# A decoder step with gathered experts: the first tile routed in four parts, the last part gathered as pairs of rows

## What is computed

```
h  = x + W_out( sigmoid(g_A) * SWA(n) + sigmoid(g_B) * GLA(n) ),   n = RMSNorm(x)
x' = h + PEER(n2),   n2 = RMSNorm(h);   then the final RMSNorm

PEER, for each token t, 8 heads:
  q      = n2 @ Wq                                  (16 sub-queries of 128)
  s      = q . sub-keys                             (16 score rows of 128)
  val,idx= top 16 of each score row
  sv     = top 16 of the pairwise sums of the two halves of a head  -> expert numbers
  g      = softmax(sv)
  out    = sum over 8 x 16 experts of  g * gelu(u[e] . n2) * v[e]
```

## Time and profile before

| | |
|---|---|
| median of 3 runs | 3785.92 us (3781.08 to 3799.24) |
| profiled execution | 3796.31 us |
| its span, first to last instruction | 3794.4 us |
| mean granted TensorE clock | 0.863 |
| busy share: TensorE matmul, VectorE, GpSimd, ScalarE | 76%, 74%, 64%, 19% |
| moved by DMA | 1298.82 MB, mean 342 GB/s |

### The profile page before, as it was taken

One profiled execution on the slowest core, in us unless ns is written; L12 is line 12 of the kernel. 1 busy time (PEld: TensorE's weight loads), 2 busy tenths in 40 slices (PEclk: granted clock), 3 DMA queues, 4 the chain that ended last, 5 costly groups with the idle time before them and its releaser, 6 DMA issues.

```text
span 3794.4 us, 33054 instructions
## 1 busy us (share of the span) xinstructions
PE 2893.8 (76%) x10012; PEld 1804.1 (48%) x10012; DVE 2803.8 (74%) x5629; ACT 726.4 (19%) x1673; POOL 2434.8 (64%) x2076
## 2 busy tenths in 40 slices
PE   8888589788787998888997768888777555555555
PEld 6777566456553665544663445455654211111111
DVE  0641788887788767877879897887889766766665
ACT  1321113322111133222121112322111110001001
POOL 0000176887667747766766777787667777777776
PEclk9899899899899997998999889988989767766668
DMA  4124399999999998999999999999999999999999
GB/s 150 45 90 171 126 403 402 349 355 405 420 401 350 412 345 313 335 348 383 387 409 349 362 344 413 394 337 378 421 406 355 351 351 362 413 385 366 373 368 364
DMA packets 342240, 1298.82 MB, mean 342 GB/s; under 512 B 39480, under 2 KB 48720, under 8 KB 321936
## 3 DMA queue, kind: packets, MB, share of 16 engines
q0 software_dynamic: 297216, 1082.26, 74.5%
q1 hardware_dynamic: 44848, 214.44, 14.6%
HBM read 1278.87 MB, written 19.76 MB: 342 GB/s over the span
## 4 chain that ended last, share of the span: by engine, by line
POOL 35%; PE 23%; DVE 15%; issue 12%; DMA 12%; DVEq 2%; ACT 1%; PEld 0%; ACTq 0%; SPq 0%; PEldq 0%; POOLq 0%
POOL ringb L600 35%; PE bank L867 9%; DMA ringb<-in_v,eidx 8%; PE vsum L777 5%; DVE ringb L1366 4%; PE bank L1064 3%; DVE acc L1408 2%; PE bank L907 2%; DVE scT L1779 1%; PE bank L923 1%; DMA wring<-in_w 1%; DMA ringb<-in_u,eidx 1%; PE bank L948 1%; DVE idx L1577 1%; DVE idx L1569 1%
## 5 line engine op out<-in xcount | busy, mean ns | idle before, releaser
L600 POOL DMA_INDIRECT ringb<-in_u,eidx x1024 | 1220.8, 1192 | 937.8 <-DVE eidx L1474 457.9
L777 PE MATMUL vsum<-ringb,diag 128*128 128x512 f32 x2164 | 1284.3, 737 | 615.2 <-DMA ringb<-in_v,eidx 567.4
L600 POOL DMA_INDIRECT ringb<-in_v,eidx x1024 | 1190.8, 1163 | 399.9 <-issue 300.0
L1366 DVE CUSTOM_DVE_ANT_0 ringb<-ringb,n2t 128x1024 f32<-128x1024 f32 x1032 | 1234.7, 1224 | 156.6 <-DMA ringb<-in_u,eidx 91.7
L777 PEld LDWEIGHTS vsum<-ringb,diag 128*128 128x128 f32 x2164 | 463.0, 229 | 1317.2 <-issue 1154.4
L1408 DVE SCALAR_TENSOR_TENSOR acc<-ringb,wgt,acc 128x1024 f32<-128x1024 f32 x483 | 620.7, 1285 | 326.6 <-DMA ringb<-in_v,eidx 315.9
L867 PE MATMUL bank<-wring,nTb 128*128 128x256 f32 x3024 | 681.4, 386 | 31.6 <-DMA wring<-in_w 28.0
L867 PEld LDWEIGHTS bank<-wring,nTb 128*128 128x128 f32 x3024 | 544.7, 182 | 171.2 <-DMA wring<-in_w 33.1
L1102 ACT ACTIVATE diag<-cst,wgt 128x128 f32<-128x128 f32 x541 | 207.6, 397 | 809.7 <-PE vsum L777 670.0
L907 PE MATMUL bank<-nTb,wring 128*128 128x256 f32 (+1 forms) x1152 | 263.0, 387 | 6.0 <-DMA wring<-in_w 3.2
L907 PEld LDWEIGHTS bank<-nTb,wring 128*128 128x128 f32 x1152 | 223.3, 194 | 59.9 <-issue 20.8
(11 more groups left out here) (254 smaller groups left out, 2276.1 us busy)
## 6 DMA issues: line engine op xcount, KB each, us to landing
wring<-in_w SPq DMA_DIRECT2D x152, 1024.0 KB, 7.8
ringb<-in_u,eidx POOLq DMA_INDIRECT x1024, 6.5
ringb<-in_v,eidx POOLq DMA_INDIRECT x1024, 6.5
n2t<-scratch_n SPq DMA_DIRECT2D x16, 512.0 KB, 7.5
oab<-in_xp SPq DMA_DIRECT2D x4, 1024.0 KB, 6.9
bTb<-in_keysT SPq DMA_DIRECT2D x4, 1024.0 KB, 11.3
vgb<-in_xp SPq DMA_DIRECT2D x4, 1024.0 KB, 8.9
scratch_h<-vgb SPq DMA_DIRECT2D x4, 1024.0 KB
```

What stands on the lines that cost most here:

```text
L600: pool.indirect_dma_start(out=ring[r], out_offset=None, in_=a["u"] if kind == "u" else a["v"], in_offset=bass.IndirectOffsetOnAxis(ap=at, ...
L777: last = mm(out[:, g * 512:(g + 1) * 512], lhs, ring[r][:, g * 512:(g + 1) * 512], start=(x == first), stop=(x == end))
L1366: v.tensor_tensor_reduce(out=ring[r], in0=ring[r], in1=n2t[:, n % 2, :], scale=1.0, scalar=0.0, op0=ALU.mult, op1=ALU.add, accum_out=dg[:, ...
```

## The change

- **Four parts.** The first tile is routed in four parts of two heads. After every fourth sub-query of block 0, VectorE runs `route_tile` and `gates` for two heads, and GpSimd may gather their experts. 20 quads (`EARLY`) run beside the rest of block 0. Block 1 then takes quads 20 to 120.
- **The late tile of block 0.** Its scores are no longer searched beside the matmuls: ScalarE copies them to `late_s`, and VectorE runs the 16 `best` of that tile at the start of block 1, beside `fm`.
- **Pieces.** The experts of tiles 6 and 7 are gathered from a new table `uv` in HBM whose rows hold `u` and `v` of one expert (8 KB). One gather brings 1 MB. There are 12 pieces: six in buffers that block 3 no longer needs (`wring` twice, `nTb`, `arena`, `qkb`, `n2t`), six in the ring. In this part the sums follow the dot products two steps behind (`SHORT`), and gelu is applied every 2 slots. Before it, six steps (`DRAIN`) carry the last 24 `v` rows of the old kind and no `u` rows.
- **h and n2 of block 3** stay in SBUF (`vog`, `oa`); their two stores and the loads `n2t` and `acc` of tiles 6 and 7 go. The sums of these tiles are made in place of `h`.
- Marks: block 3 now takes steps 248 to 386. The last step with work is 523 of a new count.

```diff
+SHORT = 2
+PIECES = 12
...
+HP = 2
+PARTS = PH // HP
+EARLY = 20
...
+WHOLE = SEG_OF[FIRST[NCH - 1]]
+QW = SEG_QUAD[WHOLE]
+XW = 2 * QW
+
+
+DRAIN = LAG // 2
+STEPS = QU + DRAIN + SHORT
+QUADS = STEPS + TAIL
+DOT_STEP = [a if a < QW else a + DRAIN for a in range(QU)]
+SUM_STEP = [a + DRAIN + SHORT if a >= QW else a + LAG if a + LAG < QW else QW + (a + LAG - QW) // 2 for a in range(QU)]
...
+SEG_GSIZE = [2 if i >= WHOLE else GROUP for i in range(len(SEGS))]
...
+    if c == 0:
+        for q in range(HC + 1):
+            out += [(("q", q), 4)] + ([(("rp", q // 4 - 1, i), 4) for i in range(3)] if q and q % 4 == 0 else [])
+        return out
...
-        return {k: 0 for k, _ in stages(c)}
-    lo = 0 if c == 1 else SEG_QUAD[SEG_OF[FIRST[c - 1]]] - MARGIN
-    hi = SEG_QUAD[SEG_OF[FIRST[c]]] - MARGIN
+        late = [k for k, _ in stages(c)]
+        late = late[late.index(("rp", 0, 2)) + 1:]
+        return {k: 1 + (EARLY - 1) * late.index(k) // len(late) if k in late else 0 for k, _ in stages(c)}
+    lo = EARLY if c == 1 else SEG_STEP[SEG_OF[FIRST[c - 1]]] - MARGIN
+    hi = SEG_STEP[SEG_OF[FIRST[c]]] - MARGIN
     total, done, out = sum(w for _, w in stages(c)), 0, {}
...
-    for c in range(1, NCH):
+    for c in range(NCH):
         last = None
         for (key, _) in stages(c):
             if last:
                 for q in range(MARKS[c][last], MARKS[c][key]):
-                    rate[q] = BY_PE[last[0]]
+                    rate[q] = BY_PE[last[0]] if c else 2.0
...
+        late_s = arena[:, 2304:2304 + HC * NK].rearrange("p (q n) -> p q n", q=HC)
+        late_tmp = bTb[:, 1920:2048].rearrange("p (t n) -> p t n", t=1)
...
+        flat = wring[:, :, :, :].rearrange("p w k c -> p (w k c)")
+        piece = [flat[:, 0:2 * D], flat[:, 2 * D:4 * D], nTb[:, 0:2 * D], arena[:, 0:2 * D], qkb[:, 0:2 * D],
+                 n2t[:, :, :].rearrange("p i d -> p (i d)")] + [ringb[:, r * D:(r + 2) * D] for r in FREED]
+        assert len(piece) == PIECES
...
-        STORES = [1 + (c == SC) for c in CC]
+        STORES = [(1 + (c == SC)) * (c < NCH - 1) for c in CC]
...
+        def sums_of(i):
+
+            R = NS if SEGS[i] == "S" else P
+            return vog[:, tile_at(SEGS[i])[1], :] if i >= WHOLE else acc[0:R, i % 2, :]
...
+            whole = q in DOTS and DOTS[q] >= QW
+            rows = [("u", 2 * DOTS[q] + j) for j in range(2)] if q in DOTS else []
+            rows += [("v", 2 * at + j) for at in SUMS[q] if at < QW for j in range(2)]
             for kind, x in rows:
                 i, k = ITEMS[x]
-                r, n = PLACE[(kind, x)]
-                if kind == "u" and k == 0:
+                if kind == "u" and i == 0 and k % (HP * TOPK) == 0:
+                    pool.wait_ge(picked.sem, picked.at((0, 0, k // (HP * TOPK))))
...
+                if whole:
+                    s, n = (x - XW) % PIECES, (x - XW) // PIECES
+                    if n:
+                        pool.wait_ge(piece_used[s], 2 * n)
+                    elif s == PIECES - RING // 2 - 1:
+                        row_used(pool, ("u", XW - 1))
+                    elif s >= PIECES - RING // 2:
+                        for r in range(2):
+                            r += FREED[s - (PIECES - RING // 2)]
+                            pool.wait_ge(slot_used[r], OLD_USES[r])
+                    pool.indirect_dma_start(out=piece[s], out_offset=None, in_=a["uv"], in_offset=place).then_inc(piece_here[s], 16)
+                    continue
...
+                        if c == 0:
+                            quads(1)
+                quads(MARKS[c][("rt", 0)] if c else EARLY)
...
+                            mm(room(pe, ("s1", c, m))[:, 0:P], qh[:, m % 2, P:2 * P], keysT[:, m, :], start=True, stop=True)\
+                                .then_inc(full.sem, full.did(("s1", c, m)))
...
+                    if c == 0 and q:
+                        copy(late_s[:, q - 1, :], ("s1", c, q - 1), filled(act, ("s1", c, q - 1))[:, 0:P])
+                        if q % 4 == 0:
+                            beside("rp", q // 4 - 1, 2)
+                            route_exp(c, 0, P, q // 4 - 1)
...
+                if i >= WHOLE:
+                    n2 = oa[:, tile_at(SEGS[i])[1], :]
...
+                    if c == 1:
+                        dve.wait_ge(late_ready, 1)
+                        for q in range(HC):
+                            best(dve, late_s[:, q, :], 1, P, 1, q, None, late_tmp)
+                            if q % 2:
+                                gap()
...
+                    best(dve, filled(dve, key), CH[c] if c else 1, P, 0, q, key, tmp)
+                    if c == 0 and q % 4 == 3:
+                        part, steps = q // 4, [0]
+                        if part == 0:
+                            dve.wait_ge(d_hs, stored(0))
+
+                        def gap_part():
+                            if steps[0] in (0, 3, 5):
+                                beside("rp", part, min(2, steps[0] // 2))
+                            steps[0] += 1
+
+                        route_tile(dve, 0, 0, P, gap_part, part)
+                        gates(dve, 0, 0, P, part)
+                if c == 0:
+                    continue
...
+                if c < NCH - 1:
+                    dve.wait_ge(d_hs, stored(c))
...
+        "uv": f(np.concatenate([x["peer_u"][0], x["peer_v"][0]], axis=1)),
```

More of the change, by code:

```diff
@@ L420, in build @@
         nT = nTb[:, :].rearrange("p (k t) -> p k t", k=KC)
+        qbT, kbT = (qkb[:, i * HB * CM:(i + 1) * HB * CM].rearrange("p (h t) -> p h t", h=HB) for i in range(2))
         vaS, kSn = vkS[:, 0, :], vkS[:, 1, :]
@@ L489, in build @@
         both = [(c, t) for c in CC for t, _ in tiles_of(c)]
+        routes = [(0, 0, part) for part in range(PARTS)] + both[1:]
         d_cst, d_par = sem("d_cst"), sem("d_par")
@@ L544, in build @@
         slot_used = [sem(f"slot_used{r}") for r in range(RING)]
+        piece_here = [sem(f"piece_here{r}") for r in range(PIECES)]
+        piece_used = [sem(f"piece_used{r}") for r in range(PIECES)]
         d_n2 = [sem(f"d_n2{i}") for i in range(2)]
@@ L614, in pool_program @@
             pool.sem_inc(init, 1)
-            for q in range(QU + LAG):
+            for q in range(STEPS):
                 pool_quad(pool, q)
@@ L754, in pe_quad @@
         def pe_quad(pe, q):
-            if not 0 <= q - LAG < QU:
-                return
             mm = nc.tensor.matmul
-            for j in range(2):
-                x = 2 * (q - LAG) + j
+            for x in [2 * at + j for at in SUMS[q] for j in range(2)]:
                 i, k = ITEMS[x]
@@ L774, in pe_quad @@
                     lhs, out = diag[:, diag_number[x] % DIAGS, :], vsum[:, :]
-                r = row_here(pe, ("v", x))
+                row = row_here(pe, ("v", x))
                 for g in range(2):
-                    last = mm(out[:, g * 512:(g + 1) * 512], lhs, ring[r][:, g * 512:(g + 1) * 512], start=(x == first), stop=(x == end))
-                last.then_inc(slot_used[r], 1)
+                    last = mm(out[:, g * 512:(g + 1) * 512], lhs, row[:, g * 512:(g + 1) * 512], start=(x == first), stop=(x == end))
+                last.then_inc(used(("v", x))[0], 1)
                 if x == end:
@@ L888, in beside @@
                 def beside(*point):
-                    if c:
-                        quads(MARKS[c][point])
+                    quads(MARKS[c][point])
                 beside("norm", 0)
@@ L1078, in pe_program @@
                         last.then_inc(full.sem, full.did(("sR", g)))
-                for i in range(12):
+                for i in range(12 if c else 0):
                     beside("rt", i)
@@ L1403, in dve_quad @@
                     dve.wait_ge(d_h[i % 2], 16 * (i // 2 + 1))
[L1404 to L1405 removed]
                 dve.wait_ge(wgt_ready, m + 1)
[L1407 to L1411 removed]
+                row, y = row_here(dve, ("v", x)), sums_of(i)
@@ L1413, in route_tile @@
+                STT(y, row, wgt[:, m % 2, at:at + 1], y, ALU.mult, ALU.add).then_inc(used(("v", x))[0], 1)
+        def route_tile(dve, c, t, R, gap, part=None):
             v = nc.vector
             TT = v.tensor_tensor
[L1415 to L1418 removed]
@@ new lines, in route_tile @@
+            scratch = small if part is None else small0
+            cut = lambda lo, n: scratch[0:R, lo * n_p:(lo + n) * n_p]
+            some = lambda lo, n: cut(lo, n).rearrange("p (a h k) -> p a h k", a=n, h=n_h)
+            xf = cut(0, 2).rearrange("p (q k) -> p q k", q=2 * n_h)
+            piu, pif, pij, e01 = some(2, 4).bitcast(u32), some(6, 4), some(10, 2), some(12, 2)
+            posu = cut(14, 1).bitcast(u32).rearrange("p (h k) -> p h k", h=n_h)
+            vv = val[0:R, t, 2 * h0:2 * (h0 + n_h), :].rearrange("p (h c) k -> p h c k", c=2)
@@ L1440, in route_tile @@
             gap()
-            for h in range(PH):
+            for h in range(n_h):
                 v.max(sv[:, h, 8:16], cd2[:, h, :])
```

245 lines of the change are left out of this document (136 added, 109 removed).

## The result

The changed kernel takes 3743.93 us in the median of four runs (3736.41 to 3753.17). The kernel before, run beside it, takes 3792.58 us (3781.08 to 3815.6). The ratio is 0.987 (0.982 to 0.991): 1.3% faster, where 3741 us and 1.2% were forecast. The total is right. It is right because two of its terms were wrong in opposite directions: the early start (A) gave nothing that can be measured, and the pieces (B) gave more than forecast, nearly twice as much in the profiled execution.

A forecast was written before the change was run, and what follows sets the result against it. The DMA engines, hardly idle once gathers start, were taken to bound the kernel, VectorE block 1. Profiled 3796.3 - 7 - 38 = 3751 us, or 3741 us against the 3785.9 median; 8 in 10 range 3690 to 3798 us.

The forecast's parts named there:

- A: Early start in block 0: gathers start 68 us earlier, most of it paid back by block 1's end; gain 7 us.
- B: Last part: 11 us from removed stores and loads, 33 from 8 KB rows, less 6 at the end; gain 38 us.
- Start of the gathers: Block 0: first gather at about 392 us, 68 us earlier; routing one part takes 9.3 us.
- End of block 0: Block 0 ends at 504 us, 44 us later than before, with 20 quads done.
- Block 1: VectorE sets it: 600 us busy plus 75 idle, taken as 680; ends at 1184 us instead of 1191.
- rival 3: Block 1 keeps 731 us, set by its engine chains; A gives -44 us, total 3792; 10%, 6% with Rival 1 too.
- A piece: Last part: each gather of 8 KB rows takes 2.66 us, 256 take 681 us for 714; gain 33 us.
- the forecast's own sign of being wrong: The forecast is wrong if block 1 takes 640 or 720 us, or a piece 2.5 or 2.8 us.
- rival 2: Last part: deep queues absorb the disturbance; a piece costs 2.47 us, B gives 87, total 3692 us; 12%.
- Rival 1: Last part: bytes bind, not packets; a piece costs 2.79 us, B gives 5, total 3774 us; 20%.
- changeover: Six DRAIN steps, and six more steps beside block 3: the DMA is full either way, so no cost.
- The end: After the last landing: 6 us longer (2 to 12), about 16 us to the end.

The follow-up runs named there:

- the half rows: Changed kernel with two gathers per piece from the joined table, each bringing only 2 KB after a buffer's first use: 1.021 of the kernel before, 3888.18 us.
- the new dot product in the last part: Changed kernel with two 4 KB gathers per piece from u and v, and scalar-tensor-tensor dot products in the last part: 0.990 of the kernel before, 3765.68 us.

## Why the forecast came true, and where it didn't

**Start of the gathers: right.** First gather at 394.6 us (392), a part's route 9.9 us (9.3). That is 66 us earlier than before.

**End of block 0: 7 us late.** The norm of block 1 starts at 512 us (504 to 505 forecast). The four routes were costed well; GpSimd and VectorE waited more for each other in between.

**Block 1: the step of A that failed.** Forecast were 600 us of VectorE's work plus 75 of its other waits, taken as 680 in all. Measured are 586.55 busy and 104.5 idle in 691 us: 85% and not over 86%. The work was put 13 us too high, and the idle time too low by 30. The waits for rows, which the sum took as gone, fell from 44.7 to 14.9 us:

```profile
DVE acc L1509 <- DMA ringb<-in_v,eidx: 12.2, 7, 3.2
DVE ringb L1464 <- DMA ringb<-in_u,eidx: 2.7, 3, 1.3
```

But the other idle time, which I had kept at 75, became 90. I had treated it as a constant of the mixer, and it isn't one: on the first chip it is 80 us for the pieces alone and 90 to 93 in the three kernels with the early start; on the third chip it is 98 without and 94 with it. That fewer quads beside the mixer leave more of VectorE's waits for TensorE and ScalarE unfilled would fit the first pair and not the second; it is not shown, and the cause stays open. The outcome lies between the forecast and rival 3, which named the mechanism (the mixer keeps part of its pace) with a block 1 of 731 us. A gave -10 us in the profiled execution, where +7 was forecast, and -5 (not distinguishable from 0) in the runs beside the pieces alone; by the traces of that pair block 1 ends 4 us later with it, on the third chip 3 us. So of 66 us of earlier start nothing measurable reached the end.

**A piece: the step of B that failed.** Forecast 2.66 us, measured 2.48 to 2.50, 426 GB/s in 560 us on end; 2.5 was the forecast's own sign of being wrong. By the forecast's own sum, 256 x (2.79 - 2.48) = 79 us in place of 33. The number is that of rival 2 (2.47), the reason is not. Rival 2 let deep queues absorb slow transfers; no slow transfers were there to absorb. I had the chain reversed: not "slow transfers hold GpSimd up while it writes descriptors", but VectorE's operations hold GpSimd, and the queues get less than they could move. A piece halves the gathers, GpSimd has 2.48 us for 1.71 of work, and with that all of the disturbance goes from 3150 us on, and not a third of it. Rival 1 (bytes bind at 2.79) fell with the half rows. The clue was in the rows: GpSimd followed itself at 0.30 us in the last part, also where the rate was low. An engine that never waits is the pace, whatever the DMA share says. (Of the four windows that the forecast put at 419 to 427 GB/s three are so, in rows 4; the one of rows 3 is 414.)

**What the sum of B missed besides.** 79 + 11 - 6 would be 84 us; about 70 came. The changeover costs about what is missing:

```profile
3066.00:3150.00 84.00, 48.44 (x79) 13.71 (x80) 55.45 (x92) 14.48 (x36) 49.44 (x32) 0.76 0.89 362
3080.00:3090.00 10.00, 7.91 (x19) 1.53 (x17) 2.01 (x2) 0.00 (x0) 3.18 (x3) 1.00 1.01 427
3100.00:3110.00 10.00, 6.12 (x10) 2.20 (x11) 9.93 (x16) 1.48 (x6) 7.95 (x2) 0.83 0.65 243
3110.00:3120.00 10.00, 3.21 (x7) 0.87 (x5) 4.55 (x9) 0.49 (x2) 8.78 (x5) 0.99 0.40 142
...
3078.39 0.94 POOL L676 DMA_INDIRECT ringb<-in_uv,eidx  x1 [5.06 <-PE vsum L857]
...
3102.83 12.36 POOL L676 DMA_INDIRECT arena<-in_uv,eidx  x1 [2.05 <-DVE vgb L1509]
...
3113.17 1.21 DVE L1464 CUSTOM_DVE_ANT_0 nTb<-nTb,oab 128x1024 f32<-128x1024 f32 x1
```

362 in place of 426 GB/s over 84 us are 13 us. Between 3073 and 3096 us GpSimd waits up to 5 us for ring buffers whose `v` rows TensorE has not yet added, but the transfers in flight cover most of that (427 GB/s from 3080 to 3090). Eleven of the 13 us lie between 3100 and 3120, and there one single gather lasts 12.36 us. VectorE, which has pieces in store, runs ten dot products and sums from 3102.49 to 3114.38 us without a break, and the gather ends 0.81 us after the last. So what the forecast missed is the same hold once more: a gather can be held through a whole unbroken run of operations. The six other traces of kernels with pieces of 8 KB each have one gather of 12.4 to 13.3 us at this place. I had put the changeover ("the DMA is full either way, nothing") at zero.

**The end: right.** From the last landing (3718.67) to the end of the span (3734.6) 16 us. GpSimd's share in the last part is 56% by its records (under 45% forecast), since gathers are held there, too.

**What bounds the last part now.** The DMA engines: their share is 1.01, VectorE waits for pieces and GpSimd for free ones.

```profile
DVE ringb L1464 <- DMA ringb<-in_uv,eidx: 71.9, 57, 2.2
POOL ringb L676 <- DVE vgb L1509: 77.6, 52, 3.8
```

**Where the forecast stood by luck.** In the profiled executions A fell short by 17 us and B was over by 32, so 45 us were forecast and 60 came. The medians show 49: the profiled execution of the changed kernel, at 3736.41 us, is the fastest of its four, 7.5 us under their median. So a 3741 that agrees to 3 us with 3744 is two opposite errors and some scatter. By the runs alone, B was worth 64 us on the first chip (3799.74 to 3736.01) for 38 forecast. That B is no constant shows on the third chip: there the pieces alone gave 95 us, and the kernels with 4 KB rows needed 1.41 to 1.44 us a row in their last part where the kernel before needed 1.39 on average in the profile of rows 2. Why the chips differ is open.

## What to carry to other kernels

Where gathers run at a steady pace, look first whether the engine that issues them ever waits. If each follows the last by its bare issue time, instructions are the pace, and rows of twice the size in half the instructions gave back here what lay above the DMA's own rate; half the bytes in as many instructions gave nothing. An earlier start of work that runs beside other stages need not reach the end: here 66 us of it didn't, and the idle time that I had subtracted as "the mixer's own" was not constant. Where an engine with work in store runs without a break, look what it keeps from the one that issues the transfers.

## Of the hardware

- An operation of VectorE over two SBUF operands holds a gather of GpSimd that begins while it runs until 0.81 us after its end; a gather that begins first takes its 0.94 us and is not disturbed. This fits 246 of 257 gathers in the last part of the kernel before, and the 0.81 us are the same for dot products of 1.23 and of 0.7 us. A reduction over one operand held none of 51. The Trainium skill, SBUF — State Buffer (Who interferes with whom), has the rule on which this bears: a VectorE instruction with two SBUF inputs contends with a GpSimd instruction that reads SBUF, and the lock on the ports that the two share is exclusive. A gather takes its indices (`eidx`) from SBUF, so by that rule the trace agrees, with the 0.81 us beside it. The same section infers that `tensor_tensor` leaves the making of descriptors alone; there the trace disagrees, since all 67 gathers that began well inside such an operation over two SBUF operands were held. That it is the reading of the indices which is held was not tried.
- The hold can outlast the operation. Of the 385 gathers above, 374 ended 0.81 us after the operation that they began beside, and 11 after a later one of an unbroken run, with up to 4.1 us for one gather. In the changeover of the changed kernel one gather was held through ten operations, 12.36 us.
- The DMA share tells little of how near to its limit the DMA is: 0.96 at 367 GB/s (two gathers from `u` and `v`), 0.99 at 377 (the kernel before), 1.01 both at 404 (the new dot product in the last part) and at 426 (the changed kernel), and 0.63 at 178 GB/s. The GB/s against the best stretch of the same kernel would have told at once that 10% were free.
- Rows of 8 KB move at 426 GB/s. Rows of 4 KB alone move at 420 at best, which is GpSimd's bare pace of 1.25 us a gather; between 4 KB rows from two tables and 4 KB halves of neighbouring rows there is no difference (3848.00 and 3848.16 us).
